# The first norm of a two-layer encoder: token factor applied to the results instead of to the input

## What is computed

```python
def rmsnorm(x, g):
    xf = xf * lax.rsqrt(jnp.mean(xf * xf, axis=-1, keepdims=True) + EPS)
    return (xf * g).astype(x.dtype)
...
hp = rmsnorm(xp, g[0])                     # D_MODEL = 1024
p = h @ w_in                               # q 512, k 128, v 128, gate_b 512, gate_c 512, hx 512 columns
q = rope_partial(q, pos); k = rope_partial(k, pos)
attn = band_attention(q, k, v, sinks)
conv_y, new_hist = causal_dwconv(gate_c * hx, sconv_hist, conv_w)     # depthwise, width 3
out = jnp.concatenate([attn, gate_b * conv_y], axis=-1) @ w_out
```

## Time and profile before

| | |
|---|---|
| time, median of 3 runs | 3106.03 us (3106.03 to 3110.19) |
| the profiled execution | 3109.17 us, span 3107.4 us |
| TensorE busy | 2969.4 us, 96% of the span, 17686 instructions |
| VectorE, ScalarE, GpSimd busy | 1382.7, 916.0, 783.5 us |
| mean granted clock | 0.975 of full speed |
| DMA | 178.32 MB, mean 57 GB/s |

### The profile page before, as it was taken

The page is one execution under the profiler, slowest core; times in us unless marked ns, Lnnn a source line. Parts: engine busy times, 40 slices in busy tenths (PEclk is TensorE's granted clock), DMA queues, the critical chain, the costliest instruction groups (busy, mean ns, idle before and its releaser), DMA issues. The chain is left out here.

```text
span 3107.4 us, 46216 instructions
## 1 busy us (share of the span) xinstructions
PE 2969.4 (96%) x17686; PEld 1771.7 (57%) x17686; DVE 1382.7 (44%) x2163; ACT 916.0 (29%) x1730; POOL 783.5 (25%) x763
## 2 busy tenths in 40 slices
PE   5899999999999999799999999999879999999997
PEld 3565565666666666455565565565445666666664
DVE  4355427222222111778659659659572222221113
ACT  4233235222222111344425325325342222221111
POOL 3010104222222000427316316317232222221001
PEclk9999999999999999898999999999989999999998
DMA  3200223111111110410120120120141111111113
GB/s 117 52 28 21 31 66 129 51 44 47 41 47 55 47 46 30 149 55 31 55 75 25 56 75 25 62 68 25 60 144 46 47 41 46 47 40 57 46 52 116
DMA packets 78970, 178.32 MB, mean 57 GB/s; under 512 B 15217, under 2 KB 43505, under 8 KB 78705
## 3 DMA queue, kind: packets, MB, share of 16 engines
q1 hardware_dynamic: 78832, 176.50, 17.8%
HBM read 147.53 MB, written 28.94 MB: 57 GB/s over the span
## 5 line engine op out<-in xcount | busy, mean ns | idle before, releaser
L149 PE MATMUL f_gu<-x_hi,w_hi 128*128 128x384 f16 x2112 | 692.4, 328 | 12.1 <-DVE x_lo L635 9.4
L150 PE MATMUL f_gu<-x_lo,w_hi 128*128 128x384 f16 x2112 | 692.5, 328 | 0.0
L151 PE MATMUL f_gu<-x_hi,w_lo 128*128 128x384 f16 x2112 | 692.0, 328 | 0.0
L133 DVE SCALAR_TENSOR_TENSOR w_lo<-w_raw,w_hi 128x1024 f16<-128x1024 f32 (+1 forms) x151 | 201.2, 1333 | 390.3 <-ACT w_hi L122 390.3
L151 PE MATMUL f_dn<-f_mid_hi,w_lo 128*128 128x384 f16 x1056 | 344.3, 326 | 0.0
L150 PE MATMUL f_dn<-f_mid_lo,w_hi 128*128 128x384 f16 x1056 | 344.3, 326 | 0.0
L149 PE MATMUL f_dn<-f_mid_hi,w_hi 128*128 128x384 f16 x1056 | 344.3, 326 | 0.0
L149 PEld LDWEIGHTS f_gu<-x_hi,w_hi 128*128 128x128 f16 x2112 | 207.4, 98 | 155.8 <-DVE x_lo L635 9.9
L150 PEld LDWEIGHTS f_gu<-x_lo,w_hi 128*128 128x128 f16 x2112 | 207.4, 98 | 140.6 <-issue 7.1
L151 PEld LDWEIGHTS f_gu<-x_hi,w_lo 128*128 128x128 f16 x2112 | 207.7, 98 | 138.6 <-issue 3.2
L122 ACT ACTIVATE w_hi<-w_raw 128x1024 f16<-128x1024 f32 (+1 forms) x151 | 167.9, 1113 | 210.0 <-PE f_dn L151 194.1
(11 more groups left out here) (373 smaller groups left out, 5494.6 us busy)
## 6 DMA issues: line engine op xcount, KB each, us to landing
w_raw<-in_gate_up SPq DMA_DIRECT2D x88, 512.0 KB, 3.5
w_raw<-in_ssm_w SPq DMA_DIRECT2D x56, 512.0 KB, 3.6
w_raw<-in_down SPq DMA_DIRECT2D x32, 704.0 KB, 4.0
mid_x<-y SPq DMA_DIRECT2D x18, 768.0 KB, 5.3
w_raw<-in_ab_w_in SPq DMA_DIRECT2D x18, 512.0 KB, 3.6
ss_state<-in_state SPq DMA_DIRECT2D x32, 256.0 KB, 3.7
out_new_state<-ss_state SPq DMA_DIRECT2D x32, 256.0 KB, 2.3
f_dn_tail_xr<-mid_x SPq DMA_DIRECT2D x8, 768.0 KB, 5.7
```

Of the source, the lines that this page charges most:

```text
L133: self.nc.vector.scalar_tensor_tensor(self.w_lo[:, u % 2, 0:cols], self.w_raw[:, u % 2, 0:cols], WSCALE, self.w_hi[:, u % 2, 0:cols], ALU. ...
L149: self.nc.tensor.matmul(out, wh, xh, start=(first and k == 0), stop=False)
L150: self.nc.tensor.matmul(out, wh, xl, start=False, stop=False)
L151: mm = self.nc.tensor.matmul(out, wl, xh, start=False, stop=(last and k == k_tiles - 1))
```

## The change

The normalized input is no longer formed. `x_hi` and `x_lo` are split from x times the gain alone, as x lands, and the token factor is put on what comes out of the projection: on the two rotation tables (they then rotate and scale q and k at once), on the values as they leave their bank (now on DVE), on gate_c with the factor squared (since gate_c and hx both carry it; the product with the kept history must be right, so it goes on the gate), and on the rows of the convolution for gate_b. `Lead` is not used here any more.

- SP loads the gains first and each half block of x in order, with the constants and rotation tables behind the third weight unit's load.
- ACT: `high(b)` and `square(b)` for each block, and all squares are kept in `squares` (24 tiles). POOL adds them in pairs (4 for a block). PE sums the pairs with the matrix of ones (128x384 results, 4 products for a block) as a hook inside the block products of the second unit. ACT takes the root of 128x384, DVE the reciprocal and two products on the tables (`factor`).
- In the mixer POOL squares the factor (`twice`) and gets a multiplication behind each gate and three behind each convolution.
- `swap` trails the block products by two instead of by one.

```diff
@@ stage_qkv
-        lead = Lead(c, ctx, "n0_lead", None, (0, 0), a["x"], None, swapped,
-                    lead_buffers(c, ctx, "n0", 0), pool_lo=2)
+        sum_bank = [c.psum(f"n0_sum{b}", [P, 512], ctx) for b in range(2)]
+        squares = c.sbuf("n0_sq", [P, BLOCKS * KD, BW], F32, ctx)
...
+            sp.dma_start(c.gains[:, :], a["norm_g"]).then_inc(gains_loaded, 16)
+            load_x(0, 0)
+            c.load_weights(sp, 0)
+            load_x(0, 1)
+            load_x(1, 0)
+            load_x(1, 1)
+            c.load_weights(sp, 1)
+            load_x(2, 0)
+            load_x(2, 1)
             c.load_weights(sp, 2)
+            sp.dma_start(c.consts[:, :], a["consts"]).then_inc(consts_loaded, 16)
+            sp.dma_start(tables[:, :, :], a["rope"]).then_inc(tables_loaded, 16)
             c.load_weights(sp, 3)
-            sp.dma_start(tables[:, :, :], a["rope"]).then_inc(tables_loaded, 16)
...
+            def sums(b):
+                def hook(k):
+                    if k % 2 == 0:
+                        return
+                    pe.wait_ge(pair_ready, KD // 2 * b + k // 2 + 1)
+                    if b == 2:
+                        pe.wait_ge(root_ready, 1)
+                    pe.matmul(sum_bank[b % 2][:, 0:BW], c.ones, squares[:, KD * b + k - 1], start=(k == 1),
+                              stop=(k == KD - 1)).then_inc(pair_used, 1)
+                return hook
...
-            lead.tensor(pe, first_unit)
+            for b in range(BLOCKS):
+                c.multiply(bank[b][:, 0:BW], s, KD, c.x_hi, c.x_lo, 0, blk(b), True, True,
+                           lambda k: pe.wait_ge(lo_ready, KD * b + k + 1)).then_inc(acc_ready, 1)
+            pe.wait_ge(consts_loaded, 16)
             swap(0)
-            swap(1)
...
-                    if m <= 3 * rot:
-                        swap(m - 1)
+                    if m < 3 * rot + 2:
+                        swap(m - 2)
...
+            act.wait_ge(gains_loaded, 16)
+            high(0, range(0, 4))
+            c.split_hi(act, 0)
+            high(0, range(4, KD))
+            square(0)
+            high(1, range(KD))
+            c.split_hi(act, 1)
+            square(1)
+            high(2, range(KD))
+            evacuate(0, 0)
+            evacuate(0, 1)
+            square(2)
+            evacuate(0, 2)
+            c.split_hi(act, s + 2, 0, acc_ready, 3)
             act.wait_ge(eps_set, 2)
+            root(0)
+            root(1)
...
+            def factor(b):
+                acc = c.acc[:, blk(b)]
+                dve.wait_ge(root_ready, b + 1)
+                nc.vector.reciprocal(acc, acc).then_inc(factor_ready, 1)
+                dve.wait_ge(factor_ready, b + 1)
+                for k in range(2):
+                    nc.vector.tensor_tensor(tables[:, k, blk(b)], tables[:, k, blk(b)], acc, ALU.mult).then_inc(scaled, 1)
...
+            for b in range(BLOCKS):
+                dve.wait_ge(acc_ready, 3 * rot + b + 1)
+                nc.vector.scalar_tensor_tensor(c.v[:, blk(b)], bank[b][:, 0:BW], 1 / WSCALE, c.acc[:, blk(b)],
+                                               ALU.mult, ALU.mult).then_inc(v_ready, 1)
+            c.split_lo(dve, s + rot + 2, 0, acc_ready, 3 * n)
@@ stage_mixer
-                        dve.wait_ge(gate_ready, BLOCKS * j + b + 1)
+                        dve.wait_ge(gate_scaled, BLOCKS * j + b + 1)
...
-                        dve.wait_ge(tap_done, 6 * (j + 1))
+                        dve.wait_ge(conv_scaled, BLOCKS * j + b + 1)
...
+                    if kind == 0:
+                        pool.wait_ge(gate_ready, BLOCKS * j + b + 1)
+                        nc.gpsimd.tensor_tensor(gate[:, blk(b)], gate[:, blk(b)], twice[:, blk(b)], ALU.mult
+                                                ).then_inc(gate_scaled, 1)
+                    if kind == 1 and b == BLOCKS - 1:
+                        pool.wait_ge(tap_done, 6 * (j + 1))
+                        for part in map(blk, range(BLOCKS)):
+                            nc.gpsimd.tensor_tensor(conv[:, j % 2, part], conv[:, j % 2, part], c.acc[:, part],
+                                                    ALU.mult).then_inc(conv_scaled, 1)
```

More of the change, by code:

```diff
@@ L1034, in _, with high @@
         @block.scalar
         def _(act):
-            act.wait_ge(eps_set, 2)
[L1037 to L1048, removed]
+            def high(b, tiles):
+                for k in tiles:
+                    act.wait_ge(x_loaded[b][2 * k // KD], 16)
+                    nc.scalar.activation(c.x_hi[:, k, blk(b)], c.y[:, k, blk(b)], AF.Copy, scale=c.gain(0, 0, k)
+                                         ).then_inc(hi_ready, 1)
@@ L1049, in _ @@
+            root(1)
+            for j in range(1, n):
+                for b in range(BLOCKS if j < rot else 0):
+                    evacuate(j, b)
+                    if j == 1 and b == 0:
+                        root(2)
                 c.split_hi(act, s + j + 2, 0, acc_ready, 3 * (j + 1))
@@ L1052, in _, with low @@
         def _(dve):
+            def low(b, tiles):
+                for k in tiles:
+                    dve.wait_ge(hi_ready, KD * b + k + 1)
+                    nc.vector.scalar_tensor_tensor(c.x_lo[:, k, blk(b)], c.y[:, k, blk(b)], c.gain(0, 0, k),
+                                                   c.x_hi[:, k, blk(b)], ALU.mult, ALU.subtract).then_inc(lo_ready, 1)
+            def factor(b):
[5 more added lines that the diff above has]
+                    nc.vector.tensor_tensor(tables[:, k, blk(b)], tables[:, k, blk(b)], acc, ALU.mult).then_inc(scaled, 1)
@@ new lines, in _ @@
+            dve.wait_ge(gains_loaded, 16)
+            low(0, range(0, 4))
+            c.split_lo(dve, 0)
+            low(0, range(4, KD))
+            low(1, range(KD))
+            c.split_lo(dve, 1)
+            low(2, range(KD))
+            c.split_lo(dve, s + 2, 0, acc_ready, 3)
+            dve.wait_ge(tables_loaded, 16)
+            dve.wait_ge(sq_ready, BLOCKS * KD)
+            for j in range(rot):
+                for b in range(BLOCKS):
+                    if j == 0:
+                        factor(b)
+                    rope(j, b)
+                if j:
+                    c.split_lo(dve, s + j + 2, 0, acc_ready, 3 * (j + 1))
@@ L1490, in convolution @@
                                                 c.cat_hi[:, 4 + j, blk(b)], ALU.subtract).then_inc(gated_lo, 1)
+            for b in range(BLOCKS):
+                pool.wait_ge(factor_ready, b + 1)
+                nc.gpsimd.tensor_tensor(twice[:, blk(b)], c.acc[:, blk(b)], c.acc[:, blk(b)], ALU.mult
+                                        ).then_inc(twice_ready, 1)
+            pool.wait_ge(twice_ready, BLOCKS)
             for i in range(len(steps) + 1):
```

94 lines of the change are left out of this document (53 added, 41 removed).

## The result

| | before | changed kernel |
|---|---|---|
| time, median of 7 runs each, measured together | 3107.83 us (3106.03 to 3110.56) | 3096.63 us (3089.62 to 3099.23) |
| the profiled execution | 3109.17 us, span 3107.4 us | 3089.62 us, span 3087.5 us |
| TensorE busy | 2969.4 us | 2965.9 us |
| GpSimd busy | 783.5 us | 800.2 us |

The ratio is 0.9964, with a 95% interval from 0.9955 to 0.9973: 11.2 us less, where 18.7 were forecast. The kernel is faster, but the time lies above the range (3081 to 3095). Its stretches tell which steps came out.

What follows compares the result with a forecast made beforehand. TensorE was taken to bound the kernel, except in the front, where it waits for the norm. 27.2 - 7.7 + 0.4 - 1.2 = 18.7 us off 3106.03 gave 3087.3 us; own range 3083 to 3092, wider range 3081 to 3095.

Steps and rivals of the forecast that it cites:

- The front, 27.2 us: Up to the first swap: TensorE no longer waits for the norm, first unit ends at 30.4 instead of 57.59 us.
- The second unit, 7.7 us: Projection's second unit: 12 f32 products with the matrix of ones, 0.64 us each, lose 7.7 us on busy TensorE.
- rival 2: Second and third projection units: factor chain too slow, one block's 5.1 us falls on TensorE, 3092.4 us; chance 8%.
- SP's queue, 0.4 us: End of projection: ScalarE's weight split no longer follows an evacuation, so SP's stores and loads move up 0.4 us.
- rival 3: Mixer's start: the gain dies because the mixer's loads land no earlier, giving 3106 us; chance 3%.
- The mixer, 1.2 us: Behind three convolutions: GpSimd products hold one small VectorE operation by about 0.4 us each, 1.2 us lost.
- the row of 0.55 us: Profile row in the mixer: a 2-element VectorE minimum took 0.55 us until the GpSimd operation beside it ended.
- The argument from PSUM: Mixer: the loss stays near the small estimate, since VectorE's copy and maximum behind the convolutions read PSUM.
- the wait of 2.87 us: TensorE wait in the mixer before the change, followed by a mean granted clock of 0.83; used to price the front.
- the 5.4 to 9 us: Mixer: expected total of TensorE's waits for prob_t in the profile after, instead of 5.4 us before.
- Rival 1: Mixer takes back more through VectorE's late places and held operations, 8 us instead of 1.2, 3094.1 us; chance 10%.
- Rival 4: Mixer: GpSimd becomes a link every block product passes, 24 operations costing 31.3 us, 3117.4 us; chance 3%.

Runs made afterwards that it cites:

- mixer_part_alone: The kernel before plus only the GpSimd products added in the mixer, by factors of one, against the kernel before: 3112.58 us, ratio 1.0009.
- after_again: The changed kernel run and profiled once more with no edit, against the kernel before: 3097.53 us, ratio 0.9959.
- front_part_alone: The changed kernel without its GpSimd work in the mixer (factor squares, gate and convolution products), against the kernel before: 3093.04 us, ratio 0.9956.
- no_conv_scaling: The changed kernel without the 12 GpSimd products on the convolution, gate products kept, against the kernel before: 3091.47 us, ratio 0.9951.

## Why the prediction came out as it did

**The front, 27.2 us: right, measured 26.3.** First swap 31.31 instead of 30.4 us. ScalarE began at 5.84 us, close to the 6.0, TensorE at 11.57 (11.6), and it waited for block 2 until 25.59 (about 25). The low clock held until 29.04 us, for about 3.5 of the block's eight tiles (3.45 us at 0.97 each), 1.6 us; I took 1.3, with four tiles as the worst case. In the five other executions with the same front the first swap came at 31.4 to 32.7 us, and in mixer_part_alone, with the front of before, at 60.0 instead of 57.6, so the 26.3 us are good to about 2.

**The second unit, 7.7 us: right.** The lead at the projection's end is 18.47 us, which is 26.3 - 7.8. Granted clock 1.00, no idle time, no wait for qkv_raw: rival 2 fell.

**SP's queue, 0.4 us: right, as far as it can be told.** The lead grows by 1.1 us until the mixer runs (18.47 to 19.63). 0.3 of it is the earlier store; TensorE's wait there fell from 11.2 to 10.2 us. That disposes of rival 3. The other 0.8 are not a fixed part of the change: in after_again the lead grows by 0.9 us there, and in the six other kernels with the new front by 0.3 to 0.9.

**The mixer, 1.2 us: this step failed; measured 7.2.** The mechanism and its places were right: three GpSimd products behind a convolution, where VectorE is late already, hold a small operation. Two things were wrong in its size. First, I let one operation be held by 0.4 us in each of three places, near the row of 0.55 us, and the waits grew by 1.06, 0.59 and 1.30 us. That row had one GpSimd operation beside it. With a row of them, each in its turn can hold the next small operation that VectorE issues. Behind the second convolution the second and third product held two operations on the path, for 0.29 and 0.75 us, and the low half behind them held a third that is not on it. The argument from PSUM held for the maxima alone (1.01 us in both kernels); the operations behind them read and write SBUF.

The Trainium skill (SBUF — State Buffer, Who interferes with whom) calls this an exclusive lock and not a shared bandwidth. This case's trace agrees (0.16 against 0.91 us for the same four elements, while a read of PSUM beside it was not held). An operation with one input in SBUF (L1396) was held as well, for 0.54 us. The prediction set that rule aside for the nearer row, and the rule had the better mechanism, but not the price: nearly 8 us were counted by it, and the waits grew by 3.0, about one GpSimd operation of 0.99 us in each place.

Second, I priced a wait by its own length. The waits grew by 3.0 us, but the lead fell by 7.2, and the 3.16 us of one stretch stand in rows with TensorE fully busy at 0.50. I had shown this myself with the wait of 2.87 us and counted it in the front alone. The waits for prob_t, 8.4 us, lie within the 5.4 to 9 us that the prediction named as its sign, while its sum had room for 6.6 only. Rival 1, with 8 us in the mixer, came close in number: 3094.1 against 3096.63. That is partly luck, since its 8 us were two whole operations in each place and no clock, where 3.0 us of waits and 4.2 of clock were measured.

**Rival 4** had the right engine but the wrong way. No wait on u or gated appeared: the products never became a link that TensorE passes. They cost by what they do to the neighbour.

**The base.** The median of before was 3106.03 us over the three runs shown and 3107.83 over the seven of the comparison. The sum by measured terms, 26.3 - 7.8 + 1.1 - 7.2 = 12.4 us, from 3107.83 gives 3095.4; measured 3096.63. The base alone moves the answer by 1.8 us. The prediction's own range was also added up loosely: from 3087.3, a front that ends at 29 us and a mixer at 0 give 3084.7 as its lower end, not 3083.

**What stays open.** Why the clock falls in some executions and not in others with the same waits: front_part_alone loses 3.3 us to it and no_conv_scaling 0.1. One profile of each kernel can't say how often. So it is open too how much of the 4.2 us belongs to the change: they are counted against one trace of the kernel before that has no low clock behind its third convolution. And no run shows what puts the SSD mixer at 981 us in some executions and at 987 to 988 in others.

## What to carry to other kernels

By these runs, work given to an idle GpSimd is free only if VectorE has nothing short and urgent to do meanwhile: look for the chain of small VectorE operations that someone already waits on, and place GpSimd's operations behind it, not beside it. Price a new wait of TensorE at its length plus the low clock that may follow, and read stretches of 3 us for it, since no view of waits shows that part. And where a change helps by moving the start of a chain, look at what else stands ahead on the same engine: here 16 squares that nobody wanted yet were worth 5 us.

## What the runs showed of the hardware

- Three GpSimd products of 128x384 f32 in a row stretch VectorE operations on four elements a partition from 0.16 to 0.91 and from 0.25 to 0.54 us; maxima that read PSUM beside them took 1.01 us with and without. They take 3.82 us there, the first of them 1.91 beside VectorE's weight split, and 2.90 us where VectorE is mostly waiting.
- The same stage with the same instructions took 981.1 us in one execution and 987.4 in another, with granted clocks of 0.84 and 0.76 over its first 60 us and 0.94 and 0.86 over its third. For changes worth 0.3% one profiled execution is no measure of the time.
- TensorE at a granted clock of 0.50 can be busy for all of 6 us behind a stretch in which it worked 1.41 of 3 us: busy time at the low clock looks like full use. Behind 2.11 and 2.09 of 3 us, with the same wait of 1.06 us, the clock fell to 0.54 in one execution and stayed at 1.00 in the other.
